# Local mixer's gates ahead of its projections in a two-layer hybrid block, with a rewritten play order

## What is computed

```
def hybrid_layer(x, ...):
    h = rms_norm_2(x, norm_g)
    proj = h @ w_in
    (q_lat, kv_lat, k_rope, g_mla, c_h, c_b, c_c, g_conv, s_q, s_k, s_v, g_swa) = jnp.split(proj, offsets, axis=-1)
    y_mla  = mla_mixer(q_lat, kv_lat, k_rope, ...) * jax.nn.silu(g_mla)          # 8 heads, rotary, causal, 512 x 512
    y_conv = short_conv_mixer(c_h, c_b, c_c, conv_w) * jax.nn.silu(g_conv)       # c_b * conv3(c_c * c_h)
    y_swa  = swa_mixer(s_q, s_k, s_v, q_norm, k_norm, sinks) * jax.nn.silu(g_swa)  # local: window of 128, four blocks
    return x + jnp.concatenate([y_mla, y_conv, y_swa], axis=-1) @ w_out
```

## Time and profile before

| what | value |
|---|---|
| median of 3 runs | 1611.1 us (1608.8 to 1611.14) |
| profiled execution | 1611.23 us, of which the instructions span 1609.4 us |
| granted TensorE clock, mean of the span | 0.964 |
| PE busy | 1488.8 us (93%) |
| DVE, ACT, POOL busy | 804.0, 585.9, 311.0 us |
| chain that ended last | PE 77%, DVE 11%, ACT 5%, POOL 3% |

### The profile page before, as it was taken

The page is one execution under the profiler, slowest core; times in us unless marked ns, Lnnn a source line. Parts: engine busy times, 40 slices in busy tenths (PEclk is TensorE's granted clock), DMA queues, the critical chain, the costliest instruction groups (busy, mean ns, idle before and its releaser), DMA issues.

```text
span 1609.4 us, 23671 instructions
## 1 busy us (share of the span) xinstructions
PE 1488.8 (93%) x10032; PEld 1151.3 (72%) x10032; DVE 804.0 (50%) x1257; ACT 585.9 (36%) x1017; POOL 311.0 (19%) x257
## 2 busy tenths in 40 slices
PE   5999797987899999999999899989899899998989
PEld 3777565875678888888876687767687678776767
DVE  7666847244643333323436555555652555554652
ACT  4255231245332222232323533432542344333431
POOL 0000133101001111000002324352300332343320
PEclk8999799989989999999998999999999999999999
DMA  9239243430212222232230121111123011111122
GB/s 358 72 110 108 72 159 121 146 119 29 90 66 92 102 94 92 92 132 97 92 120 26 40 79 66 66 53 53 53 92 112 35 58 66 66 66 47 59 68 90
DMA packets 51368, 143.11 MB, mean 89 GB/s; under 512 B 13248, under 2 KB 17984, under 8 KB 50496
## 3 DMA queue, kind: packets, MB, share of 16 engines
q1 hardware_dynamic: 51264, 141.60, 26.7%
HBM read 136.90 MB, written 4.69 MB: 88 GB/s over the span
## 4 chain that ended last, share of the span: by engine, by line
PE 77%; DVE 11%; ACT 5%; POOL 3%; issue 2%; DMA 1%; SPq 0%; DVEq 0%; POOLq 0%; ACTq 0%
PE b L407 75%; ACT arena L2206 3%; DVE arena L1267 2%; POOL arena L2865 2%; PE b L410 2%; DVE arena L1275 2%; DVE ringr L1267 1%; ACT ring L2209 1%; DVE arena L1972 1%; DVE arena L2163 1%; DVE X L1267 1%; DVE tile L1267 1%; DMA arena<-scr_yd 1%; DVE arena L1271 1%; DMA cst<-in_cst 1%
## 5 line engine op out<-in xcount | busy, mean ns | idle before, releaser
L407 PE MATMUL b<-tile,ring 128*128 128x512 f32 (+1 forms) x1840 | 661.2, 399 | 9.8 <-ACT tile L2209 7.7
L407 PEld LDWEIGHTS b<-tile,ring 128*128 128x128 f32 (+1 forms) x1840 | 347.4, 189 | 97.8 <-issue 16.2
L407 PE MATMUL b<-HR,ring 128*128 128x512 f32 (+1 forms) x944 | 387.7, 411 | 24.1 <-DVE arena L1267 13.8
L1267 DVE TENSOR_TENSOR ringr<-ring,ring 128x1024 fp32r<-128x1024 f32 x186 | 240.3, 1296 | 322.3 <-ACT ring L2209 321.2
L407 PE MATMUL b<-HR,ringr 128*128 128x512 f32 (+1 forms) x944 | 373.2, 395 | 0.0
L407 PE MATMUL b<-arena 64*64 64x64 f32 (+10 forms) x3104 | 241.5, 285 | 41.4 <-DVE arena L1278 15.4
L2209 ACT ACTIVATE ring<-ring 128x1024 fp32r<-128x1024 f32 x186 | 195.3, 1054 | 164.6 <-DMA ring<-in_ws 164.6
L407 PEld LDWEIGHTS b<-arena 64*64 64x64 f32 (+5 forms) x3104 | 153.8, 147 | 119.6 <-issue 92.1
L407 PEld LDWEIGHTS b<-HR,ring 128*128 128x128 f32 (+1 forms) x944 | 179.3, 190 | 73.1 <-issue 16.6
L407 PEld LDWEIGHTS b<-HR,ringr 128*128 128x128 f32 (+1 forms) x944 | 178.8, 189 | 45.7
L407 PE MATMUL b<-tile,ringr 128*128 128x512 f32 x448 | 179.4, 400 | 0.0
(11 more groups left out here) (131 smaller groups left out, 1259.2 us busy)
## 6 DMA issues: line engine op xcount, KB each, us to landing
ring<-in_ws SPq DMA_DIRECT2D x218, 512.0 KB, 3.5
arena<-in_ws SPq DMA_DIRECT2D x15, 512.0 KB, 15.3
arena<-in_lw SPq DMA_DIRECT2D x2, 1280.0 KB, 7.0
X<-in_xT SPq DMA_DIRECT2D x2, 1024.0 KB, 6.4
arena<-scr_kpad SPq DMA_DIRECT2D x8, 256.0 KB, 11.4
X<-in_xT SPq DMA_DIRECT2D x1, 2048.0 KB, 8.1
outT<-X SPq DMA_DIRECT2D x8, 256.0 KB, 2.0
arena<-in_cst SPq DMA_DIRECT2D x1, 1088.0 KB, 5.8
```

What stands on the lines that cost most here:

```text
L407: return self.e.matmul(out, lhsT, rhs, start=start, stop=stop, skip_group_check=True)
L1267: return self.e.tensor_tensor(out=out, in0=a, in1=b, op=op)
```

## The change

Two edits that belong together. (1) In `dense_rest` of all engines the four gate tiles of the local mixer (30 to 33, emptied by DVE's `scaled`) stand right behind the first mixer's gates, ahead of `wq` and `wkv`; the norm and transposes of the local mixer's projections, which were interleaved with those gates, are now interleaved with the first convolution tiles. (2) The string: the first two of the `q` groups take a dense tile more each, so that gates 30 and 31 lie among the rotary steps; between the heads' 24 steps stand 19 dense steps instead of 23, since several `hdx` become `hx`; two of the four now come ahead of the heads and two behind the last one. The matmuls are the same in number and kind.

```diff
--- before.py
+++ after.py
@@ -25,8 +25,8 @@
 PREP = "zpzzpz" + "smzpm" + "szpmzp" + "sssss" + "zps" + "zpss" + "zpss" + "zps" + "zps"
 MIX = ("rrrrarrrrarrrrra" + "ssssrrrrrrrra" + "sssrrrrrrrra" + "srrrrsrrrra" + "srrsrrsrrsrra" + "srrrrrrrra"
        + "rrrrasrrrrs" + "rgsrgsrsrsrrsrsr" + "ogooog")
-LAYER = ("qqqd" * 4 + "q" + "hd" * 9 + "hdx" * 3 + "hd" + "hdx" * 5 + "hd" + "hdxx" * 2 + "hdx" + "hdxx" + "hdxy" + "dx"
-         + "xddxdxdd" + "dddd")
+LAYER = ("qdqqd" * 2 + "qqqd" * 2 + "q" + "hd" * 2 + "hd" * 8 + "hdx" + "hx" + "hdx" + "hd" + "hdx" + "hx" + "hdx" * 2
+         + "hx" + "hdxx" * 2 + "hx" + "hdxx" + "hdxy" + "dxdxdd" + "ddxdxd" + "dddd")
 WINDOW = "a0 b0 r0 t0 s0 a1 b1 r1 t1 s1 a2 b2 r2 a3 b3 t2 r3 s2 t3 s3".split()
 HOME, BEFORE = [0, 0, 1, 0], [None, 0, None, 1]
 
@@ -1139,6 +1139,9 @@
         for n in range(4):
             self.proj(l, 4 + n, (act, (l, "g", n)))
             yield
+        for n in range(4):
+            self.proj(l, 30 + n, (dve, (l, "g", 8 + n)))
+            yield
         hold = [self.take((l, "wq", q)) for q in range(4)]
         for r in range(8):
             w = self.weights([(self.name, 24 + n, r) for n in range(4)], 4)
@@ -1158,28 +1161,11 @@
         for j in range(2):
             self.give((l, "wkv", j), (dve, (l, "wk", j)), (act, (l, "wv", j)))
         yield
-        gates = iter(range(4))
-
-        def gate():
-            for n in gates:
-                self.proj(l, 30 + n, (dve, (l, "g", 8 + n)))
-                break
-        for _ in range(2):
-            gate()
-            yield
-        gate()
-        yield
-        self.window_t(l)
-        gate()
-        yield
-        for j in range(4):
-            self.proj(l, 8 + j, (act, (l, "ch", j)))
-            yield
-            self.proj(l, 16 + j, (dve, (l, "cu", j)))
-            yield
-            self.proj(l, 12 + j, (dve, (l, "yc", j)))
-            yield
-            self.proj(l, 20 + j, (act, (l, "g", 4 + j)))
+        conv = self.conv(l)
+        for n in range(16):
+            next(conv)
+            if n == 2:
+                self.window_t(l)
             yield
         yield
         each = [[(k.s("y_act"), (l, "hi", r)), (k.s("y_pool") if r % 2 else k.s("y_dve"), (l, "lo", r))] for r in range(8)]
@@ -1191,6 +1177,14 @@
             self.dense(("middle", o, n), [(o, n, r) for r in range(4, 8)], k.Y[4:8], k.bank[o, n][:, :], each[4:],
                        start=False, stop=False)
             yield
+
+    def conv(self, l):
+        act, dve = self.k.s("rest_act"), self.k.s("rest_dve")
+        for j in range(4):
+            for m, emptied in ((8, (act, (l, "ch", j))), (16, (dve, (l, "cu", j))), (12, (dve, (l, "yc", j))),
+                               (20, (act, (l, "g", 4 + j)))):
+                self.proj(l, m + j, emptied)
+                yield
 
     def window_t(self, l):
         k = self.k
@@ -2060,6 +2054,10 @@
         for n in range(4):
             self.blocks(8)
             yield
+        for n in range(4):
+            self.blocks(8)
+            scaled(30 + n, k.G[:, 8 + n, :], (l, "g", 8 + n))
+            yield
         for r in range(8):
             self.blocks(4)
             if r % 2:
@@ -2074,21 +2072,16 @@
             self.cp(k.WT_[:, 2 * j:2 * j + 2, 512:640], v[:, :, 0, :]).then_inc(*dve.inc((l, "wk", j)))
         yield
 
-        def gate(n):
-            self.blocks(8)
-            scaled(30 + n, k.G[:, 8 + n, :], (l, "g", 8 + n))
-        for n, _ in enumerate(self.window_norm(l)):
-            gate(n)
-            yield
-        gate(2)
-        yield
-        gate(3)
-        yield
         CU, YC = k.CU, k.YC
         self.e.memset(CU[:, 0:2], 0.0).then_inc(*dve.inc((l, "pad")))
+        norm = self.window_norm(l)
         for j in range(4):
+            if j == 0:
+                next(norm)
             self.blocks(8)
             yield
+            if j == 0:
+                next(norm)
             self.blocks(8)
             y = YC[:, j, :]
             self.wait_ge(D, (name, 16 + j))
@@ -2769,25 +2765,19 @@
             for q in (2 * j, 2 * j + 1):
                 self.af(k.SV[:, q, :], v[:, q - 2 * j, 1, :], ACT.Copy, scale=rt[:, q:q + 1]).then_inc(*act.inc((l, "wv", j)))
         yield
-        for part in self.window_norm(l):
+        norm = self.window_norm(l)
+        for n in range(16):
+            j = n // 4
+            if n < 2:
+                next(norm)
+            elif n == 2:
+                self.window_t(l)
             self.blocks(8)
-            yield
-        self.blocks(8)
-        yield
-        self.window_t(l)
-        self.blocks(8)
-        yield
-        for j in range(4):
-            self.blocks(8)
-            self.wait_ge(dve, (l, "cu", j - 1) if j else (l, "pad"))
-            copy(8 + j, k.CH, (l, "ch", j))
-            yield
-            self.blocks(8)
-            yield
-            self.blocks(8)
-            yield
-            self.blocks(8)
-            copy(20 + j, k.G[:, 4 + j, :], (l, "g", 4 + j))
+            if n % 4 == 0:
+                self.wait_ge(dve, (l, "cu", j - 1) if j else (l, "pad"))
+                copy(8 + j, k.CH, (l, "ch", j))
+            elif n % 4 == 3:
+                copy(20 + j, k.G[:, 4 + j, :], (l, "g", 4 + j))
             yield
         self.gates(l, range(4, 12))
         yield
@@ -3032,22 +3022,21 @@
         for n in range(4):
             scaled(k.G[:, n, :], act, (l, "g", n), (l, "g", n))
             yield
-        for _ in range(6):
+        for _ in range(9):
             yield
         S = k.LST[:, 168:208].rearrange("p (q h) -> p q h", q=4)
-        for q in (1, 3):
-            v = k.WT_[:, q, :].rearrange("p (h d) -> p h d", d=64)
-            self.wait_ge(dve, (l, "winv"))
-            self.tt(v, v, S[:, q, :].unsqueeze(2).broadcast_to((128, 10, 64)), ALU.mult).then_inc(*pool.inc((l, "wn", q)))
-        yield
-        yield
-        yield
         for j in range(4):
             if j:
                 scaled(k.G[:, 3 + j, :], act, (l, "g", 3 + j), (l, "g", 3 + j))
             scaled(k.CH, act, (l, "ch", j), (l, "ch1", j))
             scaled(k.CH, pool, (l, "ch1", j), (l, "ch", j))
             yield
+            if j == 0:
+                for q in (1, 3):
+                    v = k.WT_[:, q, :].rearrange("p (h d) -> p h d", d=64)
+                    self.wait_ge(dve, (l, "winv"))
+                    self.tt(v, v, S[:, q, :].unsqueeze(2).broadcast_to((128, 10, 64)), ALU.mult).then_inc(
+                        *pool.inc((l, "wn", q)))
             self.wait_ge(dve, (l, "cu", j))
             self.ts(k.YC[:, j, :], k.CU[:, 0:512], k.pc(f"cw{l}", j), ALU.mult).then_inc(*pool.inc((l, "tap", j)))
             yield
```

## The result

The changed kernel takes 1639.9 us (median of 4 runs, 1637.8 to 1641.4), the kernel before 1611.1: a ratio of 1.018, 95% interval 1.0163 to 1.0198, slower by 28.7 us. Forecast were 1628 us, slower, with a range from 1604 to 1642. The sign and most of the places are right; the loss is 11.5 us larger than the sum, and the time lies 2 us above the range that the forecast had for itself (1616 to 1638).

A forecast was written before the change was run, and what follows sets the result against it. PE bounds the kernel, through idle time and half-speed clock, with no engine saturated. Terms sum to +8.6 us per layer, twice +17.2 on 1611.2 us, giving 1628 us, range 1604 to 1642.

The forecast's parts named there:

- rotary steps, wait: Rotary steps: PE's 2.77 us wait for block 1's query bank shrinks to 0.6 us; -2.2 us per layer.
- rotary steps, half speed: Rotary steps: the slow-clock stretch behind the 2.77 us wait goes; -1.7 us per layer.
- gate 33 ahead of `wq`: Start of `wq`: its last bank waits for DVE's multiply of gate 33; +1.3 us per layer.
- `wkv` behind A(3): `wkv` behind head 3's scores: second bank waits 3.6 us for the third exponential, before 0.6; +3.0 us per layer.
- `B(3)` behind the 20 transposes: Second bank of `B(3)`: with no tile between, PE waits for ACT's and DVE's copies, splits and multiply; +5.0 us per layer.
- local block 1, transposes: Local block 1: fewer tiles between scores and transposes, so PE waits for POOL's scaling; +3.3 us per layer.
- local block 1, product: Product with the values: DVE's copies stand behind `cu` 2 and taps; wait 7.3 us instead of 4.05, +3.2 per layer.
- behind the last heads: End of layer: extra tiles cover waits of 1.19 and 3.94 us, 0.4 of 2.40 is left; -7.1 us per layer.
- The clock: Half speed behind new waits at `wkv`, `B(3)` costs +6.2, -2.5 goes behind the last heads; +3.7 us per layer.
- heavier clock rival: Rotary half speed stays, new stretches reach their upper bound, block 1 gets a second; +15.1 per layer, 1641 us, chance 0.15.
- Catch-up: Earlier new waits let other engines draw level, so local block 1's waits vanish; -5.0 us per layer, 1601 us, chance 0.15.
- The lower ends: Gate 33, `B(3)`, block 1's transposes and the clock all at their lower bounds; +1.3 us per layer, 1614 us, chance 0.08.

The follow-up runs named there:

- thin middles: Kernels with 19 dense steps between the heads' steps: the changed kernel, 1639.9 us, and the kernel before with that spacing, its four leftover steps behind the last heads, 1603.4 us.
- five moves apart: Changed kernel with one move each: tile ahead of B(3) 1624.1 us, ahead of block 1's product 1618.2, A(3) earlier 1633.0, last transposes earlier 1628.5, gate tile 22 earlier 1630.8.
- four together: Changed kernel with tile 20 ahead of B(3), C(5) and tile 14 ahead of block 1's product, A(3) and the last transposes earlier: 1584.1 us, ratio 0.983.

## Why the prediction was right, and where it was too small

By its steps, in us per layer; the measured column is layer 0 of the changed kernel against layer 0 of before.

| step | predicted | measured |
|---|---|---|
| rotary steps, wait | -2.2 | -2.0 (0.77 left) |
| rotary steps, half speed | -1.7 | 0 |
| gate 33 ahead of `wq` | +1.3 | +1.4 |
| `wkv` behind A(3) | +3.0 | +3.2 |
| `B(3)` behind the 20 transposes | +5.0 | +5.3 (0.26 and 5.04) |
| local block 1, transposes | +3.3 | +2.9 |
| local block 1, product | +3.2 | +2.4 |
| tile 21 behind `B(5)` | not in the sum | +1.25 |
| behind the last heads | -7.1 | -4.5 (2.99 left instead of 0.4) |

The waits come to +9.9 against +6.5; the rest of the 14.5 us is 4.6 of busy time, against 2.0 of clock in the sum (3.7 less the 1.7 above). But 2.0 of the 4.6 lie ahead of the first rotary product, in 45 matmuls that the change doesn't touch; windows of before and of after:

```profile
841.15:849.16 8.01, 6.02 (x45) 5.39 (x44) 2.06 (x4) 5.00 (x10) 0.00 (x0) 0.94 0.19 65
```

```profile
841.99:851.93 9.94, 7.98 (x45) 7.52 (x43) 2.06 (x4) 4.99 (x10) 0.00 (x0) 0.70 0.15 53
```

The same 24 matmuls of one column in it took from 3.18 to 5.28 us in layer 0 of the profiled kernels. From the first rotary product on it is 2.6 us of clock against 2.0, and 12.6 us in all against 8.6. In layer 1 the same part took 6.80 us instead of 5.32. So in these two executions 3.4 of the 11.5 us above the forecast are no effect of the change, as far as the profiles tell; some 7 are waits.

*Right, and shown by a run of its own:* `wkv` (A(3) moved), `B(3)` (one tile ahead of it), the order of DVE at local block 1 (`cu` 2 and its taps ahead of the copies, as the prediction has it; another order of the tiles in this one group takes 5.7 of the 6.46 us away), and POOL's scaling, for which PE waits 2.9 us in the thin middles and 0.6 when C(5) lies over it. So the two waits at local block 1 have two causes: POOL's comes from fewer tiles, the longer one from the kind of tile that the new order of gates moved there. The longer one was put at 7.3 us and measured 6.46 though the product came no sooner than forecast: 9.52 us behind the first transpose against 9.2. The prediction took 1.9 us for the transposes between; at half speed they took 3.06.

*The tail was mis-sized.* "the gates and splits that DVE and ACT did in between now come earlier, 0.4 is left": they do come earlier, but not early enough. DVE did four multiplies, a weight split and two splits of the output (3.46 us for two) ahead of the copies, and before the change the last of these stood behind them. The step should have listed what DVE has queued between the transposes and the copies, as it did in the middle. 2.6 us.

*Tile 21 was left out.* `hx` in place of `hdx` also put a tile 5.7 us sooner behind `A(6)`, whose first exponentials it needs for its bank. 1.25 us.

*The clock.* The prediction took half speed to follow a wait of over 2.7 us, and none of 2.07. In the changed kernel one wait of 2.07 us was followed by it, in both layers. Layer 0 begins with the same instructions up to here in runs with other middles; here are 7.00 us behind each of the two waits of 2.07 us, first in the run with the tile ahead of B(3), then in that with the tile ahead of the product:

```profile
892.86:899.86 7.00, 7.00 (x29) 5.43 (x30) 4.65 (x8) 0.58 (x1) 3.41 (x5) 1.00 0.06 8
906.80:913.80 7.00, 7.00 (x24) 5.59 (x25) 4.22 (x7) 0.57 (x1) 2.83 (x4) 0.76 0.00 0
```

```profile
894.77:901.77 7.00, 7.00 (x29) 5.42 (x30) 4.65 (x8) 0.58 (x1) 3.40 (x5) 1.00 0.04 5
908.71:915.71 7.00, 7.00 (x37) 5.91 (x38) 4.65 (x8) 0.85 (x2) 2.84 (x4) 1.00 0.03 4
```

In the changed kernel behind the first, here behind the second, and behind neither: the same wait costs 1.6 us or nothing. The profiles of all ten kernels with the new order of gates have twenty such layers: behind the first wait 15 times, behind the second twice, in three layers behind neither. With the old order (three kernels, six layers) half speed followed the wait of 2.77 us every time and the twelve of 2.07 behind it once. So taking the 2.77 us away mostly moved the half-speed stretch to the next wait. The Trainium skill, "TensorE: Matmul & The Clock Gate", part 1 on the clock gate, says that the hardware's look at PE's activity is not tied to where the kernel starts, so that the point of change varies between runs of the same kernel. The traces agree, with one profiled execution each of kernels that are the same up to there. A gain of 1.7 us for this wait was there in three of the twenty layers. The heavier clock rival had part of this right: the half-speed stretch among the rotary steps stayed, and local block 1 has two of them on end (clock 0.52 over 14 us; with gate tile 22 there, and 5.7 us less idle, the same 14 us run at 0.76). Of the new waits, 3.78 us cost 1.3 us of slow matmuls (`wkv` is busy 12.89 us instead of 11.59), less than the 3.1 that the prediction took from the one place where it had a row; part of each stretch lies inside the wait.

*The rivals.* Catch-up is refuted: its 5 us per layer would need waits that vanish when others arise, and five moves apart and four together show that they don't. POOL's wait at local block 1 is 2.88 or 2.89 us whatever was taken away ahead of it; the product's wait comes out longer where the transposes ran faster (7.07 us for 6.46 with A(3) moved, 7.58 in layer 1 of the run with the last transposes moved), and from the first transpose to the product it is 9.5 us each time. The lower ends didn't come together: gate 33, `wkv` and `B(3)` came out above the values taken, the two at local block 1 somewhat below, and the clock above its sum. The measured time lies some 1 us from the heavier clock rival's 1641, and that is luck: the rival's 13 us more were to be clock alone, and measured it is mostly waits. The rule of the Trainium skill, "SBUF — State Buffer", section "SBUF: two separate sides", on the port that DVE and POOL share, would have given 1631 us with a DVE split behind POOL's scaling. The rows bear it out as a mechanism: at local block 1 the split next to POOL's 3.60 us took 1.72 us instead of 1.23, and behind the last heads one took 4.03 us next to POOL's 4.47:

```profile
1148.95 4.03 DVE L1261 TENSOR_TENSOR ringr<-ring,ring 128x1024 fp32r<-128x1024 f32 x1
```

```profile
1147.43 4.47 POOL L2855 TENSOR_TENSOR arena<-arena 128x2048 f32<-128x2048 f32 x1 [1.97 <-DVE arena L2168]
```

Neither split lay on the path: at local block 1 DVE idles 5.1 us for the tap right behind it, and behind the heads it waits 2.65 us for ACT. But the step of POOL that stood beside the first of them did:

```profile
1087.54 1.57 POOL L2858 TENSOR_SCALAR arena<-arena 128x128 f32<-128x128 f32 x1
```

This first scaling of `P(7)` took 1.57 us where its shape takes 0.73 on average, `P(7)` as a whole 5.24 instead of 4.78, and POOL's tap, the taps and the copies stand behind it. So at local block 1 POOL's long step and the split cost this path 0.8 us by that row, 0.5 of it new against before, and not 1.2. How much of the tail's 3.46 us for two splits of 512 columns is the port isn't shown; no run took POOL's pair, which runs beside them, away. In the run with the gate tile moved POOL's multiplies beside DVE's four are on the path there, 1.9 us.

## What to carry over

Where one string sets the order of all engines, moving work by two steps changes which kind of step stands ahead of each chain on the in-order engines, and at local block 1 that weighed more than how many tiles cover it (5.7 us against 2.9): write down, for every result that PE waits for, the full queue of the engine that makes it, and look for a step that itself waits for a third engine (here DVE's taps for POOL). Waits at different places proved independent, so they could be mended one at a time and their savings added; at one place, local block 1, taking one wait away brought another until both causes were mended. A tile of filler is worth most between a row of transposes and the next step that needs their result or their banks. What a single wait of 2 to 3 us costs in clock is known only on the average of several executions.

## What the runs showed of the chip that was not expected

- A wait of 2.07 us behind 16 transposes was followed by half speed in some executions and not in others, with the same instructions around it (18 of 52 in the profiles). A wait of 2.88 us likewise: in the run with the tile ahead of the product the clock was 1.00 over the 14 us behind it in layer 0, and 0.88 in layer 1.
- Two waits close together (2.88 and 6.46 us with 16 transposes between them) gave nearly 14 us of half speed on end, of which PE was busy for 7.54.
- POOL's multiply of 2048 elements took 3.60 to 4.47 us, and its four scalings before `B(7)` 5.24 us where they took 4.78 before; DVE's durations moved more: its split of 128x1024 took 1.23 us by itself and 4.03 beside POOL's 4.47.
